# Where the normalised input and the activation rows begin in SBUF, relative to the split weights

## The reference, cut to what matters

```python
for i in range(DEPTH):                       # DEPTH = 2
    mod = (c_act @ ada_w[i] + ada_b[i])[:, None, :]
    sh_a, sc_a, g_a, sh_f, sc_f, g_f = jnp.split(mod, 6, axis=-1)
    h = rms_norm(x, norm_g[i, 0]) * (1.0 + sc_a) + sh_a
    y = moba_attention(...) if i % 2 == 0 else diff_attention(...)
    x = x + g_a * rms_norm(y, norm_g[i, 1])
    h = rms_norm(x, norm_g[i, 2]) * (1.0 + sc_f) + sh_f
    x = x + g_f * rms_norm(swiglu(h, ffn_w_in[i], ffn_w_out[i]), norm_g[i, 3])
...
def swiglu(h, w_in, w_out):                  # w_in 1024 x 5632, w_out 2816 x 1024
    g, u = jnp.split(h @ w_in, 2, axis=-1)
    return (jax.nn.silu(g) * u) @ w_out
...
def conformer_conv_module(h, w1, b1, dw_w, dw_b, ln_g, ln_b, w2, b2):
    a, gt = jnp.split(h @ w1 + b1, 2, axis=-1)
    u = causal_dwconv(a * jax.nn.sigmoid(gt), dw_w) + dw_b      # width 31
    return jax.nn.silu(layernorm(u, ln_g, ln_b)) @ w2 + b2
```

## The kernel before

| tensor | begins, modulo 512 | distance to the weights, modulo 512 |
|---|---|---|
| `h_hi`, `h_lo` | 192 | 64 |
| `ab_hi` row 0 | 192 | 64 |
| `ab_hi` row 1 | 312 | 184 |
| `ab_lo` row 0 | 448 | 320 |
| `ab_lo` row 1 | 56 | 440 |
| `mix` | 192 | 64 |
| `ident`, `ones` | 448 | 320 |

## Time and profile before

### The profile page before, as it was taken

One profiled execution on the slowest core, in us unless ns is written; L12 is line 12 of the kernel. 1 busy time (PEld: TensorE's weight loads), 2 busy tenths in 40 slices (PEclk: granted clock), 3 DMA queues, 4 the chain that ended last, 5 costly groups with the idle time before them and its releaser, 6 DMA issues. The chain is left out here.

```text
span 995.7 us, 19019 instructions
## 1 busy us (share of the span) xinstructions
PE 963.3 (97%) x6806; PEld 886.0 (89%) x6806; DVE 821.5 (83%) x1217; ACT 543.3 (55%) x1023; POOL 77.9 (8%) x111
## 2 busy tenths in 40 slices
PE   4899999999999999998999999999999999999997
PEld 3899988999999888996999999989997899999996
DVE  4869978887777778777988777789998989987885
ACT  3455546544444467555644444459998555555452
POOL 2100002000000012011300000002240000000000
PEclk9999999999999999999999999999999999999999
DMA  9999973999999965652599999985340649766641
GB/s 347 327 339 336 337 256 108 349 348 318 312 312 310 285 190 162 179 176 79 174 354 347 317 312 308 314 258 170 86 127 1 201 133 286 225 187 183 183 121 42
DMA packets 240770, 234.08 MB, mean 235 GB/s; under 512 B 7497, under 2 KB 208970, under 8 KB 240714
## 3 DMA queue, kind: packets, MB, share of 16 engines
q1 hardware_dynamic: 237824, 226.52, 73.8%
q0 software_dynamic: 1616, 5.32, 1.6%
q10 hardware_dynamic: 1274, 1.52, 0.4%
HBM read 232.27 MB, written 1.06 MB: 234 GB/s over the span
## 5 line engine op out<-in xcount | busy, mean ns | idle before, releaser
L1341 DVE TENSOR_TENSOR wlo<-raw,whi 128x1024 fp32r<-128x1024 f32 x286 | 346.7, 1222 | 67.4 <-ACT whi L999 67.2
L527 PE MATMUL work<-h_hi,whi 128*128 128x256 f32 x1360 | 383.1, 282 | 2.0 <-DVE h_lo L1402 1.9
L527 PE MATMUL work<-h_hi,wlo 128*128 128x256 f32 x1360 | 381.0, 280 | 0.0
L527 PE MATMUL work<-h_lo,whi 128*128 128x256 f32 x1360 | 380.8, 280 | 0.0
L999 ACT ACTIVATE whi<-raw 128x1024 fp32r<-128x1024 f32 x286 | 297.7, 1053 | 143.5 <-PE work L527 45.4
L527 PEld LDWEIGHTS work<-h_hi,whi 128*128 128x128 f32 x1360 | 256.5, 189 | 5.4 <-issue 2.0
L527 PEld LDWEIGHTS work<-h_lo,whi 128*128 128x128 f32 x1360 | 256.1, 188 | 3.1
L527 PEld LDWEIGHTS work<-h_hi,wlo 128*128 128x128 f32 x1360 | 257.0, 189 | 0.0
L1351 DVE SCALAR_TENSOR_TENSOR acc<-ada_raw,csil,acc 128x1024 f32 (+1 forms) x128 | 163.7, 1280 | 6.1 <-DMA ada_raw<-in_ada_w 4.4
L564 PE MATMUL Y<-whi,ab_hi 128*128 128x512 f32 x286 | 90.0, 395 | 0.0
L564 PE MATMUL Y<-whi,ab_lo 128*128 128x512 f32 x286 | 89.8, 395 | 0.0
(11 more groups left out here) (226 smaller groups left out, 1323.8 us busy)
## 6 DMA issues: line engine op xcount, KB each, us to landing
ada_raw<-in_ada_w SPq DMA_DIRECT2D x88, 512.0 KB, 6.5
raw<-in_ffn_w_in SPq DMA_DIRECT2D x88, 512.0 KB, 7.6
ada_raw<-in_mod_w SPq DMA_DIRECT2D x48, 512.0 KB, 6.8
raw<-in_ffn_w_out SPq DMA_DIRECT2D x44, 512.0 KB, 5.7
raw<-in_f_up_w SPq DMA_DIRECT2D x44, 512.0 KB, 4.0
raw<-in_moba_w_qkv SPq DMA_DIRECT2D x24, 512.0 KB, 8.3
raw<-in_diff_w_qkv SPq DMA_DIRECT2D x24, 512.0 KB, 7.8
raw<-in_a_pw_w SPq DMA_DIRECT2D x24, 512.0 KB, 6.5
```

Of the source, the lines that this page charges most:

```text
L527: mm = pe.matmul(dst, w[:, u, ws], h[:, k, :], start=(k == 0 and m == 0), stop=(k == KT - 1 and m == 2))
L1341: dve.tensor_tensor(wlo[:, u, :], raw[:, u, :], whi[:, u, :].bitcast(F32), ALU.subtract).then_inc(lo[u], 1)
```

## The change

The two pairs of activation rows become four tensors of their own, and small tensors and two spacers are put between them so that each begins at 384 modulo 512. Some small tensors (192 bytes in all) are allocated ahead of `h_hi`, so that `h_hi` and `h_lo` also begin at 384. The weights stay at 128. `taps`, the convolution's per-row coefficients, becomes one tensor for each row. No instruction is added, removed or moved on any engine; operands have other addresses.

| tensor | before, modulo 512 | after | distance to the weights before | after |
|---|---|---|---|---|
| `h_hi`, `h_lo` | 192 | 384 | 64 | 256 |
| row 0 of hi, of lo | 192, 448 | 384 | 64, 320 | 256 |
| row 1 of hi, of lo | 312, 56 | 384 | 184, 440 | 256 |
| `head_bias`, `Ga`, `Gf` | 192 | 384 | 64 | 256 |
| `mix` | 192 | 0 | 64 | 384 |
| `ident`, `ones` | 448 | 64 | 320 | 448 |

```diff
+        csil = sb("csil", [P, 16])
+        relt = sb("relt", [32, H])
+        colA = sb("colA", [P, KT])
+        colB = sb("colB", [P, KT])
+        ssy = sb("ssy", [P, 2 * TT])
         h_hi = sb("h_hi", [P, KT, S], F32R)
         h_lo = sb("h_lo", [P, KT, S], F32R)
         head_bias = sb("head_bias", [P, H, REL])
         Ga = sb("Ga", [P, D])
         Gf = sb("Gf", [P, D])
-        ab_hi = sb("ab_hi", [P, 2, PADW], F32R)
-        ab_lo = sb("ab_lo", [P, 2, PADW], F32R)
+        ab_hi0 = sb("ab_hi0", [P, PADW], F32R)
+        small = sb("small", [P, 96])
+        ab_hi1 = sb("ab_hi1", [P, PADW], F32R)
+        taps0 = sb("taps0", [P, 72])
+        sb("spacer21", [P, 24])
+        ab_lo0 = sb("ab_lo0", [P, PADW], F32R)
+        taps1 = sb("taps1", [P, 72])
+        sb("spacer24", [P, 24])
+        ab_lo1 = sb("ab_lo1", [P, PADW], F32R)
         mix = sb("mix", [P, 2692])
         cols = sb("cols", [P, COLS])
-        csil = sb("csil", [P, 16])
-        colA = sb("colA", [P, KT])
-        colB = sb("colB", [P, KT])
-        taps = sb("taps", [P, 2, 72])
...
-        a_hi, a_lo = ab_hi[:, :, 0:S], ab_lo[:, :, 0:S]
-        u_hi, u_lo = ab_hi, ab_lo
+        u_hi, u_lo, taps = (ab_hi0, ab_hi1), (ab_lo0, ab_lo1), (taps0, taps1)
+        a_hi, a_lo = ([row[:, 0:S] for row in rows] for rows in (u_hi, u_lo))
...
-                    row_product(a_hi[:, j, :], a_lo[:, j, :], 4 + j, i + nb2, first)
+                    row_product(a_hi[j], a_lo[j], 4 + j, i + nb2, first)
...
-                            mm = pe.matmul(Y[:, j, 0:S], diag[w][:, m, :], u[:, j, m:m + S],
+                            mm = pe.matmul(Y[:, j, 0:S], diag[w][:, m, :], u[j][:, m:m + S],
```

More of the change, by code:

```diff
@@ L755, in w_o @@
                     pe.wait_ge(alo, i * 2 + (rb + j + 1))
-                    row_product(a_hi[:, j, :], a_lo[:, j, :], 6 + j, i + nb3, first, end, half_way)
+                    row_product(a_hi[j], a_lo[j], 6 + j, i + nb3, first, end, half_way)
                 lag = 2 if s == 0 else 3
@@ L761, in w_o_quarter @@
                     pe.wait_ge(alo, i * 2 + (rb + j + 1))
-                    row_quarter(a_hi[:, j, :], a_lo[:, j, :], 6 + j, i + nb3, 0, first)
+                    row_quarter(a_hi[j], a_lo[j], 6 + j, i + nb3, 0, first)
                 def w_o_rest(i, j, first):
-                    row_quarter(a_hi[:, j, :], a_lo[:, j, :], 6 + j, i + nb3, 1, first)
-                    row_tile(a_hi[:, j, :], a_lo[:, j, :], 6 + j, i + nb3, 1, first)
+                    row_quarter(a_hi[j], a_lo[j], 6 + j, i + nb3, 1, first)
+                    row_tile(a_hi[j], a_lo[j], 6 + j, i + nb3, 1, first)
                 def step(i, j):
@@ L1119, in out_hi @@
                     need(act, used[6 + j], i + nb3)
-                    act.activation(a_hi[:, j, :], src, ACT.Copy, scale=by).then_inc(ahi, 1)
+                    act.activation(a_hi[j], src, ACT.Copy, scale=by).then_inc(ahi, 1)
                 def squares(T):
@@ L1203, in step @@
                         act.wait_ge(taps_ready, i * 2 + (3 * KT + j + 1))
-                        act.activation(gate[:, j, :], work[:, 2 * j, 0:S], ACT.Identity, scale=taps[:, j, 4:5],
-                                       bias=taps[:, j, 6:7]).then_inc(cv_g0, 1)
+                        act.activation(gate[:, j, :], work[:, 2 * j, 0:S], ACT.Identity, scale=taps[j][:, 4:5],
+                                       bias=taps[j][:, 6:7]).then_inc(cv_g0, 1)
                         if more:
@@ L1219, in step @@
                     need(act, used[4 + j], i + nb2)
-                    act.activation(a_hi[:, j, :], act32[:, j, :], ACT.Copy).then_inc(ahi, 1)
+                    act.activation(a_hi[j], act32[:, j, :], ACT.Copy).then_inc(ahi, 1)
                     if more and late:
@@ L1245, in diags @@
                                 d = act.activation(diag[w][:, m, :], ident[:], ACT.Copy,
-                                                   scale=taps[:, j, 36 + w * NP + m:37 + w * NP + m])
+                                                   scale=taps[j][:, 36 + w * NP + m:37 + w * NP + m])
                             d.then_inc(diag_done, 1)
@@ L1258, in step @@
                     act.activation(gate[:, j, :], work[:, 2 * j + 1, 0:S], ACT.Sigmoid,
-                                   bias=taps[:, j, 32:33]).then_inc(gate_done, 1)
+                                   bias=taps[j][:, 32:33]).then_inc(gate_done, 1)
                     if T == 4:
@@ L1268, in step @@
                     need(act, diag_used, T * NP - NP)
-                    act.activation(u_hi[:, j, :], upad[:, j, :], ACT.Copy).then_inc(uhi, 1)
+                    act.activation(u_hi[j][:], upad[:, j, :], ACT.Copy).then_inc(uhi, 1)
                     diags(ahead, NP)
@@ L1655, in step @@
                     if s == 5:
-                        dve.tensor_scalar(taps[:, j, 0:8].rearrange("p (a g t) -> p a g t", a=4, g=2),
+                        dve.tensor_scalar(taps[j][:, 0:8].rearrange("p (a g t) -> p a g t", a=4, g=2),
                                           fdw[:, :, :, bass.ds(i * 2 + j, 1)], 1.0, None,
@@ L1669, in step @@
                         dve.wait_ge(cv_g0, t1)
-                        dve.scalar_tensor_tensor(gt[:, 1:S], g[:, 0:S - 1], taps[:, j, 2:3], gt[:, 1:S],
+                        dve.scalar_tensor_tensor(gt[:, 1:S], g[:, 0:S - 1], taps[j][:, 2:3], gt[:, 1:S],
                                                  ALU.mult, ALU.add).then_inc(cv_seq, 1)
@@ L1764, in step @@
                     u = upad[:, j, :]
-                    dve.scalar_tensor_tensor(u[:, CONV - 1:PADW], work[:, 2 * j, 0:S], taps[:, j, 31:32],
+                    dve.scalar_tensor_tensor(u[:, CONV - 1:PADW], work[:, 2 * j, 0:S], taps[j][:, 31:32],
                                              gate[:, j, :], ALU.add, ALU.mult).then_inc(act_done, 1)
@@ L1777, in step @@
                             low()
-                        w = taps[:, j, m:m + 1]
+                        w = taps[j][:, m:m + 1]
                         sums = cacc[:, c % 2, :]
                         if c == 0:
-                            v = dve.tensor_scalar(sums, u[:, m:m + S], w, taps[:, j, 33:34], ALU.mult, ALU.add)
+                            v = dve.tensor_scalar(sums, u[:, m:m + S], w, taps[j][:, 33:34], ALU.mult, ALU.add)
                         elif c == 1 and T > 3:
```

29 lines of the change are left out of this document (13 added, 16 removed).

## The result

The changed kernel takes 1003.9 us (median of four runs, 1003.11 to 1004.23) against 997.1 before: a ratio of 1.0063, with a 95% interval of 1.0051 to 1.0075. It is 0.6% slower. The profiled execution has a span of 1001.3 us against 995.7, 5.6 us more. The change adds five lines above the products, so L527 is now L532, L545 is L550, L564 is L569, L700 is L705 and L750 is L755.

The account below looks back on a forecast made before the run. PE's matmul pitch was taken to bound the feed-forward stages. Column products 16.4 us plus row products 2.7, less 0.4, gave 18.7 us off 997.55: 978.9, as a median 978.5 us; range 946 to 1008.

Parts of the forecast that it names:

- What bounds the kernel: PE alone sets the time in feed-forward stages, busy 140.00 of 140.00 us; in the conformer neither PE nor DVE alone.
- Address matters: Matmul pitch on PE depends on operand places: j=1 row products take 2.78 us against 2.80, shifted conformer windows up to 123 ns.
- the rule against it: The skill's separate SBUF read ports for moving operand and weight load, by which no distance matters and the change does nothing.
- nothing changes: Rival, 0.27: distance counts only modulo 64 or 128 bytes or not at all; L527 stays at 117.7 ns, time 997.5 us.
- Which way: At 256 bytes the reads meet less often, so L527's groups of 48 go from 5.65 to 5.45 us; chance 0.33.
- The weight loads of 140 ns: Float32 loads at 256 bytes, `ident` moving over `mix`, shorter than the usual 188 ns; taken as a hint for 256.
- The bare 429 ns: Start-to-start time of 512-column float32 matmuls at distance 192 or 256, 2.3 ns beside the columns; taken as favouring 256.
- 184 on one side, 320 on the other: Row-product distances nearest 256, neither free of read cost: 2.78 us per 12 with j=1, 2.80 with j=0.
- The four fast stretches: Stretches of 96 matmuls each, at 113.5 ns against 117.7 at the same addresses, taken as the pace 256 bytes would give.
- The slower rival: Rival, 0.23: at L527 reads meet at multiples of 128 or 256 bytes; 120 ns gives 1012.7 us, 123 ns 1027.
- The price of parting entirely: Rival, 0.17: reads never meet at 256; 109.0 ns for 256 columns, 215.6 for 512; time 944, perhaps 950 us.
- Small costs: Some 150 transposes may lose short loads, 0.4 us at most; j=1 row products may lose 0.7 us; `taps` costs nothing.

Follow-up runs that it names:

- the map: A kernel that only times matmuls on an otherwise idle core, with h at 32 distances from the weights: 113.3 to 120.1 ns for 256 columns.

## Why the prediction was wrong, point by point

**What bounds the kernel: right.** PE's pitch sets the time in the feed-forward stages, and a change of the pitch by 2 ns passed into the span: +5.7 us in the account, +5.6 in the span.

**Address matters: right, and what was drawn from the rule against it was wrong here.** The Trainium skill, "TensorE: Matmul & The Clock Gate", section "Step-by-step: what each phase is for", gives the weight load a read port of its own that takes nothing from the running matmul. The prediction drew from it that no distance matters. The trace does not agree: behind the same one-column matmul the pitch goes from 113.3 to 120.1 ns as `h` moves. Whether the two reads take anything from each other, or the cost arises otherwise, no run shows. The rival "nothing changes" (0.27) fell with it. Its argument was right for the rows it used: 64 and 320 are alike, as all pairs 256 bytes apart are in the map.

**Which way: wrong, and this is the step that failed.** The prediction took a group of 48 from 5.65 to 5.45 us at a distance of 256, -16.4 us in all. The runs show 5.75 us in its place, 120.0 ns in the map and among its slowest, which is +10.3 us over all column products. The time lies in the stated range only because the range also covered the rival that is slower. I chose the fast pace at 256 for three reasons, and none carried. The weight loads of 140 ns are the transposes' own: with their distance now 64 instead of 256 they are as short as ever.

```profile
L705 PEld LDWEIGHTS work<-ident,mix x48: 137/140/143, 57.3 to 459.1; 128*128 128x128 f32 x48
```

The bare 429 ns of float32 matmuls did not carry over to float32r ones, which pass 512 columns in 215.8 ns with the moving operand fixed and in 226.7 at the best distance. And "184 on one side, 320 on the other" set 256 between two neighbours on a line; the map is not one, with 113.3 ns at 112 and 120.0 at 128. The hint in the earlier trace rows was that 320 acts as 64. Read so, 256 would be 0, for which no row existed, and both directions would have had the same weight.

**The four fast stretches: right that the same instructions can run faster, wrong in what they were taken for.** A pace can be open at a distance and not be taken: at 64 behind a row product it never was, in 24 of 24. It goes with how a product is entered and was no sign of what another distance would give.

**The slower rival (0.23): the right place and price, and half a rule.** It said that reads meet at L527 when the distance is a whole multiple of 128 or 256, and priced it at 120 ns, 9.9 + 2.5 us for the column products. The runs show 120.0 ns at 0 and at 128, and 8.4 + 0.4 + 1.5 = 10.3 us. But 80 and 96 are no such multiples and are as slow, 120.1 ns, so the rule of multiples isn't the cause, and that its price came out so near is in part luck. Its term for the row products had the wrong sign: +2.7 expected, -4.0 measured, since they are among their best at 0. So 1012.7 became 1003.9.

**The price of parting entirely: 109.0 ns was out of reach.** With a load of 128 columns the steady pitch was never under 111.6 ns. For 512 columns the estimate of 215.6 was right (215.8 with the moving operand fixed), but no distance reached it, 226.7 being the best.

**Small costs.** Transposes kept their load, so nothing was lost there. The 0.7 us that j=1 rows would lose did not come up, since all rows gained. The count of 512-column matmuls was 12 too low (L558 has 72, not 60), which changes the sum by 0.03 us.

## What to carry to other kernels

In float32r products of 256 moving columns with a load of 128, the place of the moving operand relative to the stationary one is worth up to 6% of the pitch, and in this kernel, which PE bounds, 1.3% of the time. It costs nothing to set. Run the real order of matmuls at 16 distances in one small kernel, then take the distance that is fast behind every entry, not the fastest one seen. With 192 moving columns there was nothing to gain: the load set 111.7 ns at 0 and at 192 alike. A pace that the profile shows for some products and not for others at the same addresses tells that more than the distance decides. It is no sign for another layout, and it need not be the same from run to run, as the kernel with all at 192 shows. Choose the distance for each kind of product, and then test the kinds in turn: rows at 0 and `h` at 192, each at its best by itself, gave slow column products.

## What the runs showed of the hardware that I had not expected

- The pitch of float32r matmuls depends on the distance between moving and stationary operand modulo 256 bytes: 113.3 to 120.1 ns for 256 columns, where distances 256 bytes apart agree to 0.2 ns, and 226.7 to 234.2 for 512, where twelve matmuls agree to 0.03 us. Shifting both operands together by 64, 128 or 192 bytes left 120.0 at 0 and 117.8 at 64.
- At 192 bytes there are two paces, 113.3 and 117.8 ns. Each is kept for a whole product, and what stands ahead has a part in which it is. Where the same pair of distances gave now one and now the other, what picks it is open.
- A weight load of 128 columns allows a matmul each 111.7 ns; with 32 stationary and 128 moving columns it is 60.0, and 55.8 with both operands fixed. The extra time disappears when the moving operand is read from one column. When the stationary one is, it shrinks at a distance of 0 (from 120.0 to 113.3 ns) and stays at 192 (116.7). Why it remains with 32 stationary columns (120.0 at distance 0), and why a matmul of 512 columns pays 11 to 18 ns where one of 256 pays 2 to 8, is open: no run separates the two reads in time, so that they meet in a part of SBUF is argued and not shown.
